# Expert sums by eight 32x32 matmuls on the diagonal's blocks instead of two 128x128 ones

## What is computed

```python
q = (h @ w_q)                               # 8 heads, 2 halves of 128
s1, s2 = q[..., 0, :] @ k1.T, q[..., 1, :] @ k2.T
...                                         # top 16 of each, top 16 of their sums
g = softmax(top_s)
u = take(u_tab, idx)                        # [token, 8*16, 1024]
a = gelu(einsum('ted,td->te', u, h))
vv = take(v_tab, idx)
y = einsum('te,ted->td', g * a, vv)
```

## Time and profile before

| | |
|---|---|
| median of 3 runs | 4355.37 us (4354.42 to 4359.99) |
| span of the profiled execution, first to last instruction | 4341.7 us |
| TensorE busy | 3659.4 us, 84% |
| VectorE busy | 2777.5 us, 64% |
| ScalarE busy | 1620.4 us, 37% |
| GpSimd busy | 1442.2 us, 33% |
| DMA moved | 1569.57 MB, 362 GB/s over the span |
| mean granted TensorE clock | 0.958 |

### The profile page before, as it was taken

The page is one execution under the profiler, slowest core; times in us unless marked ns, Lnnn a source line. Parts: engine busy times, 40 slices in busy tenths (PEclk is TensorE's granted clock), DMA queues, the critical chain, the costliest instruction groups (busy, mean ns, idle before and its releaser), DMA issues.

```text
span 4341.7 us, 42866 instructions
## 1 busy us (share of the span) xinstructions
PE 3659.4 (84%) x11886; PEld 1730.5 (40%) x11886; DVE 2777.5 (64%) x6996; ACT 1620.4 (37%) x4856; POOL 1442.2 (33%) x1337
## 2 busy tenths in 40 slices
PE   5997988888888889898888888988888887888886
PEld 2444533333434344355333443453333334343332
DVE  2227666777776667546766676366767755766675
ACT  0124144444444444332444443124444431444443
POOL 0000243444444444301444443014444431444442
PEclk7998999999999999999999999999999999999999
DMA  6335699999999999974999999659999995999997
GB/s 237 138 134 195 244 421 421 422 419 408 421 415 421 417 417 399 400 282 193 421 421 421 420 409 377 254 217 420 421 421 420 407 381 229 411 421 421 421 411 332
DMA packets 207216, 1569.57 MB, mean 362 GB/s; under 512 B 23072, under 2 KB 23200, under 8 KB 30592
## 3 DMA queue, kind: packets, MB, share of 16 engines
q0 software_dynamic: 191952, 1370.57, 76.5%
q1 hardware_dynamic: 14832, 196.06, 11.5%
q10 hardware_dynamic: 192, 0.20, 0.0%
HBM read 1565.50 MB, written 1.25 MB: 361 GB/s over the span
## 4 chain that ended last, share of the span: by engine, by line
DMA 44%; PE 28%; DVE 9%; ACT 6%; issue 3%; DVEq 1%; POOL 1%; ACTq 0%; POOLq 0%; SPq 0%
DMA arena<-uv,idx 43%; PE banks L1008 16%; DVE arena L2126 4%; PE banks L557 4%; PE banks L675 2%; ACT diag L1323 1%; DMA weight_ring<-weights 1%; PE banks L590 1%; ACT wgt L1321 1%; ACT L1319 1%; ACT L1106 1%; POOL arena L504 1%; ACT gel L1319 1%; PE banks L847 1%; PE banks L571 1%
## 5 line engine op out<-in xcount | busy, mean ns | idle before, releaser
L1008 PE MATMUL banks<-arena,diag 128*128 128x512 f32 x5120 | 2500.8, 625 | 516.0 <-ACT diag L1323 511.4
L504 POOL DMA_INDIRECT arena<-uv,idx x1280 | 1413.1, 1104 | 2167.9 <-PE banks L1008 1761.8
L2126 DVE CUSTOM_DVE_ANT_0 arena<-arena 128x1024 f32<-128x1024 f32 x1280 | 1566.3, 1224 | 849.1 <-DMA arena<-uv,idx 834.6
L1008 PEld LDWEIGHTS banks<-arena,diag 128*128 128x128 f32 x5120 | 928.7, 195 | 1919.7 <-ACT diag L1323 1134.8
L1319 ACT ACTIVATE gel<-dot 128x1 f32<-128x1 f32 x1280 | 258.6, 202 | 1647.5 <-DVE dot L2126 1645.9
L1323 ACT ACTIVATE diag<-consts_sb,wgt 128x128 f32<-128x128 f32 x1280 | 514.1, 402 | 93.3 <-issue 6.6
L1321 ACT ACTIVATE wgt<-gel,gate 128x1 f32<-128x1 f32 x1280 | 376.8, 294 | 89.1 <-issue 1.4
L557 PE MATMUL banks<-weight_ring,arena 128*128 128x512 f32 (+2 forms) x812 | 350.6, 591 | 10.8 <-DMA weight_ring<-weights 7.5
L557 PEld LDWEIGHTS banks<-weight_ring,arena 128*128 128x128 f32 x812 | 153.8, 191 | 198.7 <-issue 178.8
L481 POOL DMA_DIRECT2D row_ring<-mods x34 | 18.6, 556 | 581.4 <-DMA mods<-diag 255.6
L675 PEld LDWEIGHTS banks<-arena,weight_ring 128*128 128x128 f32 x1408 | 171.5, 193 | 40.2 <-issue 39.9
(11 more groups left out here) (265 smaller groups left out, 2372.8 us busy)
## 6 DMA issues: line engine op xcount, KB each, us to landing
weight_ring<-weights SPq DMA_DIRECT2D x67, 2048.0 KB, 7.9
arena<-weights SPq DMA_DIRECT2D x18, 2048.0 KB, 11.7
arena<-uv,idx POOLq DMA_INDIRECT x1280
row_ring<-mods POOLq DMA_DIRECT2D x34, 512.0 KB, 13.6
row_ring<-gains POOLq DMA_DIRECT2D x18, 512.0 KB, 13.9
arena<-keys SPq DMA_DIRECT2D x4, 1024.0 KB, 13.5
weight_ring<-weights SPq DMA_DIRECT2D x2, 1536.0 KB, 14.0
arena<-weights SPq DMA_DIRECT2D x3, 1024.0 KB, 9.8
```

The lines of the kernel that those rows point to most:

```text
L504: pool.indirect_dma_start(out=ring[:, RING_SLOT[k], :], out_offset=None, in_=A[f"uv{l}"], in_offset=bass.IndirectOffsetOnAxis(ap=idx[:, UN ...
L1008: ins = mm_(bank[:, yb, :], diag[:, s, :], ring[:, s, D + hf * 512:D + hf * 512 + 512], start=first, stop=last, skip_group_check=True)
L2126: sig(V.tensor_tensor_reduce(out=ring[:, s, 0:D], in0=ring[:, s, 0:D], in1=xnat_of(u[0], u[1]), scale=1.0, scalar=0.0, op0=ALU.mult, op1=A ...
```

## The change

The identity that ScalarE scales is replaced by `fold`, a constant of 128x32 with a one where the column is the partition modulo 32. Scaled, it holds the four 32x32 blocks of the diagonal, one above the other. TensorE multiplies block a (partitions a to a + 31, a = 0, 32, 64, 96) with the same partitions of v. The first half's result goes to the same partitions of bank 2i. The second half's goes 32 partitions further on, modulo 128, in bank 2i + 1, so that the eight matmuls lie on eight different 32x32 tiles of the array. The residual undoes the rotation: a product over 128x512 for the first half, and four over 32x512 for the second, each of which reads the bank and the gate row at one quarter and writes another. The addition to H is as before, in a function of its own. `modst` gets memory of its own, and `diag` shrinks from 128 to 32 columns a slot.

```diff
+PT = 32
...
+CT = dict(ident=(0, 128), tri=(128, 256), win=(384, 256), cos=(640, 64), sin=(704, 64), iota=(768, 16), sel=(784, 512),
+          fold=(1296, PT))
+CT_COLS = 1296 + PT
...
-        diag = sb("diag", [P, SLOTS, P])
-
-        modst = diag[:, :, :].rearrange("p s c -> p (s c)").rearrange("p (a b) -> p a b", a=2)
+        diag = sb("diag", [P, SLOTS, PT])
+        modst = sb("mods_staged", [P, 2, 512])
...
-                        ins = mm_(bank[:, yb, :], diag[:, s, :], ring[:, s, D + hf * 512:D + hf * 512 + 512],
-                                  start=first, stop=last, skip_group_check=True)
+                        for a in range(0, P, PT):
+                            o = (a + hf * PT) % P
+                            ins = mm_(bank[o:o + PT, yb, :], diag[a:a + PT, s, :],
+                                      ring[a:a + PT, s, D + hf * 512:D + hf * 512 + 512], start=first, stop=last, skip_group_check=True)
...
-                    AF(diag[:, s, :], ident, ACT.Copy, scale=wgt[:, s:s + 1]).then_inc(sems["act"], done("act", ("diag", k)))
+                    AF(diag[:, s, :], fold, ACT.Copy, scale=wgt[:, s:s + 1]).then_inc(sems["act"], done("act", ("diag", k)))
...
-                    y = bank[:, 2 * i:2 * i + 2, :].rearrange("p a b -> p (a b)")
...
-                    residual(y, t, 0, D, g, xnat_of(r, i), evs, l >= 2)
+                    tmp_ = xnat_of(r, i)
+                    V.tensor_tensor(tmp_[:, 0:512], bank[:, 2 * i, :], g[:, 0:512], ALU.mult)
+                    for a in range(0, P, PT):
+                        o = (a + PT) % P
+                        V.tensor_tensor(tmp_[a:a + PT, 512:D], bank[o:o + PT, 2 * i + 1, :], g[o:o + PT, 512:D], ALU.mult)
+                    dve.drain()
+                    add_in(H[:, t, :], tmp_, evs, l >= 2)
...
+    at("fold")[:] = p % PT == np.arange(PT)[None]
```

More of the change, by code:

```diff
@@ L127 @@
 RSLOTS = 5
-CT = dict(ident=(0, 128), tri=(128, 256), win=(384, 256), cos=(640, 64), sin=(704, 64), iota=(768, 16), sel=(784, 512))
-CT_COLS = 1296
+CT = dict(ident=(0, 128), tri=(128, 256), win=(384, 256), cos=(640, 64), sin=(704, 64), iota=(768, 16), sel=(784, 512),
+          fold=(1296, PT))
+CT_COLS = 1296 + PT
 PT_ = dict(conv_w=(0, 12), conv_b=(12, 4), gate_b=(16, 16), lam=(32, 256), sink=(288, 16), pool_scale=(304, 8),
@@ L378, in program @@
         ident = const("ident")
+        fold = const("fold")
         ring = arena[:, RING:RING + SLOTS * 2 * D].rearrange("p (s c) -> p s c", s=SLOTS)
@@ L1638, in residual, with add_in @@
                     dve.drain()
-                    x = H[:, t, c0:c1]
+                    add_in(H[:, t, c0:c1], tmp_, events, post)
+                def add_in(x, tmp_, events, post):
                     if post:
```

## The result

The changed kernel takes **4357.6 us** (median of 20 runs, 4348.6 to 4369.6) beside 4351.6 us for the kernel before on the same chip (20 runs, 4342.8 to 4366.8). The ratio is 1.0018, with a 95% interval of 1.0010 to 1.0027: slower by 7.8 us, between 4 and 12. The forecast was slower by 15.4. The profiled execution's span grew from 4341.7 to 4346.8 us; it was the fastest of the 20 (4348.6 us), so stages are compared by it and times by the 20.

The account below looks back on a forecast made before the run. The prediction took DMA, flat at 421 to 422 GB/s in the gathers, as the bound. 0 + 3 - 0.3 + 6.0 + 4.7 + 2 = +15.4 us on the 4341.7 us span, plus 13.7 to the median, gave 4371 us; range 4357 to 4392.

Parts of the forecast that it names:

- Step 1: Each gather's eight matmuls on TensorE: two steps for all eight, 1.06 us at full clock.
- Step 2: TensorE's clock: 1.2 GHz in most of each round, because matmuls use part of the array; +3 us (-8 to +15).
- Step 3: ScalarE's diagonal with 32 columns: 320 ns, hidden but for each layer's last gather; -0.3 us.
- Step 4: VectorE's residual: five operations of 3.2 us in all replace one, +2.0 us each, three bare ones; +6.0 us.
- Step 5: Fetch of 30,720 more instructions: 1.97 MB more on the DMA engines; +4.7 us (0 if it fell where they idle).
- Step 6: Mixers after the rounds: the next mixer starts at clock 0.50 instead of 1.0; +2 us (0 to +9).
- the kept clock: Rival: TensorE's clock stays at 2.4 GHz, a gather takes 1.06 us; -1.2 us, 4354 us; chance 0.22.
- The change does less than it says: Rival: same times, only the residual and instruction fetch count; +10 us, 4366 us; chance 0.03.
- a fuller ring: Rival: the ring of gather slots no longer runs low, 20 of 36 us return; about 4342 us; chance 0.10.
- The queue of eight steps: Rival: a gather's tiles queue on TensorE, eight steps, 3.43 us or more; 5560 us at the least; chance 0.05.

Follow-up runs that it names:

- unrotated_timed: The changed kernel without the rotation (both halves on the same four tiles) and with one residual product, timed with 12 runs: 4350.6 us, ratio 0.9998.
- few_columns: The changed kernel plus one unread matmul of 128 rows x 32 columns ahead of each gather's eight: 4360.7 us in one run.
- few_rows: The changed kernel plus one unread matmul of 32 rows x 128 columns ahead of each gather's eight: 4555.6 us in one run.
- unrotated: The changed kernel without the rotation (both halves on the same four tiles) and with one residual product, first timing: 4358.3 us in one run.
- blocks64: The changed kernel with 64x64 blocks instead of 32x32, four matmuls a gather, residual in three products: 4351.9 us, ratio 1.0001.
- no_unrotate: The changed kernel with the residual as one product over 128x1024, the second half's rotation not undone: 4351.3 us, ratio 0.9998.
- split_at_ends: The kernel before with the residual in five products only for the four tiles at the layers' ends: 4358.2 us, ratio 1.0018.

## Why the prediction came out as it did

**The bound** was right: 416 to 419 GB/s before and 416 to 418 after, with 610 us of TensorE's busy time gone.

**Step 1, the matmuls:** right, 1.06 us forecast, 1.09 and 1.96 us measured. Of the Trainium skill, "TensorE: Matmul & The Clock Gate", Part 3 (row and column tiles compose) agrees with the 1.09 us. "TensorEngine Tiling (Array Packing)", Gotcha 1, differs: the first half's four row tiles write one PSUM bank, in four quadrants, and all eight matmuls still take two steps. For tiles that differ in rows and columns alike the measurement decides against the page.

**Step 2, the clock:** the mean fell to 0.77 to 0.81, which is 1.2 GHz in about 0.4 of the time, where I had "most of each round". The reason was wrong, and the rows that misled me were the earlier trace rows: 64-row matmuls, few rows and part of the array at once. unrotated_timed keeps 0.99 with 4 tiles of 16, and few_columns keeps it where few_rows loses it with as many tiles. The reading would have given the wrong answer for unrotated and for few_columns. What the kernels show is this: with two steps a gather on all rows the mean clock is 0.81 to 0.82, on 8 of 16 tiles (the change) and on all 16 (blocks64) alike; with four steps on all rows it is 0.95 to 0.96; with two steps on all rows and two on a quarter of them it is 0.88, and from 4405 to 4530 us, where it stands at 0.50, TensorE has no gap. So what goes with the low clock of the change is the fewer microseconds of work for each gather, and not the tiles. The price, +3 us, was too high as far as can be told: the stretches came out 3.1 us shorter in the profile, and the kernel without the new residual lies between -5.2 and +3.9 us with steps 2, 3, 5 and 6 all in it. That the halved steps win nothing was right, but it needs no clock: DMA is the bound at either level (no_unrotate and unrotated_timed, 0.9998 both).

**Step 3, the diagonal:** 320 ns forecast, 321 measured. Its -0.3 us is too small to see in a time.

**Step 4, the residual:** the mechanism right and its size nearly so. 3.2 us for five operations forecast, 3.49 measured; three bare ones +6.0 forecast, +6.8 by the chain, 7.8 (2 to 13) by split_at_ends. Taking nothing off for fewer partitions was right: 687 ns over 32 against 685 over 128. This term is the whole of the loss that can be seen: with it alone 1.0018 to 1.0024, without it 0.9998.

**Step 5, instruction fetch:** the step that failed. It put 1.97 MB "on the engines that are the bound" as +4.7 us. The bytes came to the digit (1.54 to 3.51 MB on q8), the time did not: unrotated_timed carries them all at 0.9998, at most +3.5 us. The step's own lower bound, 0, was the value to take, though not for the reason it gave, that the fetch falls where the engines idle: nearly all of it falls in the four stretches. These leave 36 us unused at 422 GB/s. That the fetch goes into those gaps is argued, not shown.

**Step 6, after a round:** +2 us forecast, and not found as a cost of the change. Line 559 took 9.36 us for its first 16 records behind layer 0, against 7.13 us that 16 records take at 2.4 GHz. But in the same place the same line takes longer still in split_at_ends, whose rounds run at the high clock:

```profile
1833.32 10.07 PE L557 MATMUL banks<-weight_ring,arena 128*128 128x512 f32 x16 [3.09 <-DMA weight_ring<-weights]
```

Behind layer 2 the first 16 records took 9.94 us in the change against 8.83 before, and the wait for the norm behind them covers that. In the total the step can't be told from nothing (-0.9 us for all but the residual).

**The sum.** Steps 2, 3, 5 and 6 were 3 - 0.3 + 4.7 + 2 = +9.4 us and measured -0.9 (-5.2 to +3.9); step 4 was +6.0 and measured 6.8. So 15.4 should have been about 6 to 7, which the 7.8 (4 to 12) holds. The largest single miss is the fetch, 4.7 us put where at most 3.5 and most likely nothing was. It is not the only one: with the fetch at nothing, steps 2, 3 and 6 were still put at +4.7, above the +3.9 that no_unrotate allows, so the allowances for the clock were too high as well. The forecast was too high for that, and by a little more for its base: the median of three runs lay 13.7 us above the profiled span, the median of twenty 9.9. The 4357.6 lies just inside the forecast's own range of 4357 to 4392, but that range was narrower below than its parts: with the bounds given in steps 2, 5 and 6 together it would reach 17.7 us down, not 14.

Of the rivals, the kept clock did not occur. "The change does less than it says" had +10 us from the residual and the fetch, and only the residual was there. The 20 us that a fuller ring should have given back did not come: the stretches show 3.1, about what kernels with the same matmuls differ by. The queue of eight steps did not occur, as step 1 shows.

What stays open: how the rows in use are counted, why the fetch costs nothing that can be seen, and whether the 3.1 us of the stretches are more than scatter.

## What to carry to other kernels

Where a stage is bound by DMA, a matmul that is twice as quick gives nothing; look instead at what the new layout asks of the engine that stands at the stage's end, and count only the places where it is bare, here three of ten. Splitting one VectorE operation over partitions multiplies its cost, because each part costs as much as the whole (687 and 685 ns here). And if a stretch's clock matters, shape small matmuls so that they use all rows: of two kernels that add one with equally many tiles, the one with 128 rows and 32 columns held a clock of 0.96, and the one with 32 rows and 128 columns was 195 us slower, in one run each.

## What the runs showed of the hardware that was not expected

- Neither the share of the array nor being busy alone kept the clock up: 4 of 16 tiles at a time with all 128 rows for 1.7 us a gather kept 0.99; eight tiles for 0.9 us gave 0.82 and the whole array for 0.9 us 0.81; few_rows stood at 0.50 from 4405 to 4530 us while TensorE had no gap.
- A clock that fell in TensorE's wait is paid for behind it: after 3.81 us of waiting line 557's 32 records took 16.95 us, and after 1.76 us 13.97.
- Eight 32x32 tiles, two on each group of rows and two on each group of columns, with four row tiles in one PSUM bank, run as two steps: 1.09 us, against 1.92 for the same eight matmuls on four tiles.
- VectorE takes 687 ns for 32x512 and 685 ns for 128x512 out of PSUM.
- 1.97 MB more of instructions, 2.3 times as many bytes on q8 as before, nearly all in the gathers' stretches, cost nothing that 12 runs can show (at most 3.5 us), though DMA is the bound there.
- In few_rows two shapes alternate: from 1513.50 to 1514.55 us is 1.05 us for two steps of 0.43 us, so a change of shape costs some 0.2 us, an estimate; in the changed kernel two gathers of the same shape in line start 0.86 to 0.88 us apart.

```profile
1513.50 1.12 PE L1004 MATMUL banks<-arena,consts_sb 32*128 32x512 f32 x2
1514.55 1.09 PE L1013 MATMUL banks<-arena,diag 32*32 32x512 f32 x16
```
